# L2 norms of q and k: from the chunk loop of a gated DeltaNet block into its convolution stage

## The reference

```
proj = rms_norm(x) @ w_in
qkv  = silu(causal_depthwise_conv(concat(gq, gk, gv), conv_w))      # 4 taps
cq   = l2_normalize(q per head);  ck = l2_normalize(k per head)     # x * rsqrt(sum(x*x) + 1e-6)
g    = -exp(a_log) * softplus(ga + dt_bias);  beta = sigmoid(gb)
# in chunks, per head: decay = exp(differences of cumsum(g)), lower triangle
a_mat = I + strict_lower((k*beta) @ k.T * decay);  [u, w] = solve(a_mat, [v*beta, k*beta*exp(gc)])
v_new = u - w @ S;  o = (q*exp(gc)) @ S + lower(q @ k.T * decay) @ v_new
S     = S * exp(g_last) + (k * exp(g_last - gc)).T @ v_new
o_a   = o * rsqrt(mean(o*o) + 1e-6) * gdn_norm_w * silu(gz)
```

## Time and profile before

| | before |
|---|---|
| median of 3 runs | 1145.51 us |
| profiled execution, its own time | 1145.67 us |
| its span (first to last instruction) | 1143.9 us |
| PE busy | 1130.5 us (99%) |
| POOL / DVE / ACT busy | 540.0 / 526.8 / 454.2 us |
| mean granted TensorE clock | 0.998 of full |

### The profile page before, as it was taken

One profiled execution on the slowest core, in us unless ns is written; L12 is line 12 of the kernel. 1 busy time (PEld: TensorE's weight loads), 2 busy tenths in 40 slices (PEclk: granted clock), 3 DMA queues, 4 the chain that ended last, 5 costly groups with the idle time before them and its releaser, 6 DMA issues.

```text
span 1143.9 us, 16670 instructions
## 1 busy us (share of the span) xinstructions
PE 1130.5 (99%) x5955; PEld 948.3 (83%) x5955; DVE 526.8 (46%) x1136; ACT 454.2 (40%) x747; POOL 540.0 (47%) x326
## 2 busy tenths in 40 slices
PE   9999999999999999999999999999999999999997
PEld 8778888888888888888888888887888888888886
DVE  5344356464738257777777573413333333320001
ACT  6354453534444355555555432234332223221112
POOL 5344465362626165555555544434444444434443
PEclk9999999999999999999999999999999999999999
DMA  7233333131313254443444363532333333222231
GB/s 209 78 90 95 106 92 104 56 101 50 100 56 94 73 145 124 126 127 117 123 126 122 106 225 94 146 88 80 104 97 92 93 103 98 92 92 92 92 111 74
DMA packets 176177, 119.91 MB, mean 105 GB/s; under 512 B 6657, under 2 KB 164466, under 8 KB 176130
## 3 DMA queue, kind: packets, MB, share of 16 engines
q1 hardware_dynamic: 163088, 98.20, 29.5%
q10 hardware_dynamic: 13042, 21.07, 5.8%
HBM read 110.83 MB, written 8.42 MB: 104 GB/s over the span
## 4 chain that ended last, share of the span: by engine, by line
PE 87%; DVE 5%; issue 3%; POOL 2%; ACT 1%; DMA 1%; DVEq 0%; SPq 0%; POOLq 0%; ACTq 0%
PE ps L1542 62%; PE ps L1970 10%; PE ps L1650 6%; PE ps L1502 3%; PE ps L1862 2%; POOL w_lo L567 1%; PE ps L1833 1%; PE ps L1832 1%; DVE ps L1235 1%; DVE prod L1245 1%; PE ps L1906 1%; DVE Wb L1250 1%; DMA x_nat<-in_x 1%; PE ps L1592 0%; POOL rn L562 0%
## 5 line engine op out<-in xcount | busy, mean ns | idle before, releaser
L567 POOL TENSOR_TENSOR w_lo<-raw,w_hi 128x1024 fp32r<-128x1024 f32 x169 | 414.5, 2453 | 513.6 <-ACT w_hi L709 513.6
L1542 PE MATMUL ps<-h_hi,w_hi 128*128 128x512 f32 x976 | 384.1, 394 | 1.0 <-POOL w_lo L567 1.0
L1542 PE MATMUL ps<-h_lo,w_hi 128*128 128x512 f32 x976 | 383.0, 392 | 0.0
L1542 PE MATMUL ps<-h_hi,w_lo 128*128 128x512 f32 x976 | 382.7, 392 | 0.0
L709 ACT ACTIVATE w_hi<-raw 128x1024 fp32r<-128x1024 f32 x169 | 179.3, 1061 | 474.9 <-PE ps L1542 366.2
L1542 PEld LDWEIGHTS ps<-h_hi,w_hi 128*128 128x128 f32 x976 | 183.4, 188 | 38.8 <-issue 1.9
L1542 PEld LDWEIGHTS ps<-h_hi,w_lo 128*128 128x128 f32 x976 | 183.4, 188 | 37.7 <-issue 0.2
L1542 PEld LDWEIGHTS ps<-h_lo,w_hi 128*128 128x128 f32 x976 | 183.5, 188 | 36.1
L1111 DVE SCALAR_TENSOR_TENSOR tmp<-ps,prm,tmp 128x511 f32<-128x511 f32 (+2 forms) x72 | 53.9, 749 | 78.7 <-ACT tmp L745 73.4
L1065 DVE TENSOR_SCALAR ms<-ss 128x1 f32<-128x1 f32 x8 | 1.2, 153 | 123.5 <-ACT raw L1038 117.4
L1458 DVE TENSOR_TENSOR f_lo<-tmp,f_hi 128x512 f32 (+1 forms) x22 | 40.5, 1842 | 33.6 <-ACT f_hi L1011 33.6
(11 more groups left out here) (281 smaller groups left out, 1572.0 us busy)
## 6 DMA issues: line engine op xcount, KB each, us to landing
raw<-in_w_in SPq DMA_DIRECT2D x79, 512.0 KB, 3.8
raw<-in_w_gate SPq DMA_DIRECT2D x22, 512.0 KB, 3.7
raw<-in_w_up SPq DMA_DIRECT2D x22, 512.0 KB, 3.7
raw<-in_w_down SPq DMA_DIRECT2D x22, 512.0 KB, 3.4
gate_dram<-gate ACTq DMA_DIRECT2D x24, 256.0 KB, 2.0
cum<-cum_dram ACTq DMA_DIRECT2D x8, 512.0 KB, 7.4
raw<-in_w_branch_a SPq DMA_DIRECT2D x8, 512.0 KB, 4.4
raw<-in_w_branch_b SPq DMA_DIRECT2D x8, 512.0 KB, 4.0
```

Of the source, the lines that this page charges most:

```text
L567: pool.tensor_tensor(w_lo[:, r % 2, :], raw[:, r, :], w_hi[:, r % 2, :], ALU.subtract)\
L1542: return pe.matmul(ps[:, bank, :], wts[wl][k], acts[xl][:, k, :], start=(n == 0), stop=(n == len(PASSES) - 1))
```

## The change

Squares and sums of q and k are worked out while the convolution runs, for all 512 tokens, and without transposing q and k by PE:

- For units 0 to 15 (q and k), one unit late: behind the seed of unit u, ACT squares `qkv[:, u-1, :]` (128x512, into a buffer that alternates); behind the taps of unit u, DVE transposes it in blocks of 32x32 and sums each block row (128x512 to 128x16). Sixteen such results stand side by side in `sq_part`, 128x256.
- Before unit 18, PE multiplies `sq_part` once by four stacked 32x32 identities (`eye32`), which adds up the four block rows of each head: 32x256. After the taps of unit 19, DVE adds 1e-6 in four instructions, one for each 32 partitions, and puts them in place: `nsum`, 128 x 64 (4 chunks, 16 heads of q and k).
- POOL raises `nsum` to -1/2 in eight instructions of 128x8, all in the convolution stage. `decay_rows(0)` moves to behind the low part of unit 16.
- In the chunks, the transposes of q, the squares, the sums and the two powers are gone; bn, bn2 and c1 are made once for all chunks. k is transposed in chunks 0 to 2 only (for `Kd`).
- ACT's gate exponentials move from behind the SiLU of unit 5 to behind the seed of unit 6.
- The loops over the last units of the convolution on PE, ACT and DVE are written out.

```diff
# POOL
-            units(QKV0 + 1, NCONV // 4 - 1)
-            low_part(GATE0, 0)
-            low_part(GATE0, 1)
+            def row_powers(n):
+                pool.wait_ge(norm_ready, TT)
+                power(rn[:, n * H:(n + 1) * H], nsum[:, n * H:(n + 1) * H], H).then_inc(row_pow, 1)
+            units(QKV0 + 1, 3)
+            for r in range(4):
+                low_part(QKV0 + 4, r)
+                if r == 0:
+                    pool.wait_ge(g_split, 3)
+                    decay_rows(0)
+            for r in range(4):
+                low_part(QKV0 + 5, r)
+                row_powers(r)
+            low_part(GATE0, 0)
+            for n in range(4, 2 * TT):
+                row_powers(n)
+            low_part(GATE0, 1)
...
-            pool.wait_ge(g_split, 3)
-            decay_rows(0)
             ahead(0)
             decay_mask(0)
...
-                pool.wait_ge(k_sums, c + 1)
-                power(rn[:, H:2 * H], nsum[:, H:2 * H], H).then_inc(rk_ready, 1)
                 pool.wait_ge(masked, c + 1)
-                pool.wait_ge(row_step, c * 3 + 2)
-                pool.tensor_tensor(Eb[:, :, :], E[:, :, :], heads(bn2[:, :]), ALU.mult).then_inc(Eb_ready, 1)
+                pool.wait_ge(row_step, 2)
+                pool.tensor_tensor(Eb[:, :, :], E[:, :, :], heads(bn2[:, c * H:c * H + H]), ALU.mult)\
+                    .then_inc(Eb_ready, 1)
                 ahead(n - 1)
-                pool.wait_ge(q_sums, c + 1)
-                power(rn[:, 0:H], nsum[:, 0:H], H).then_inc(rq_ready, 1)
                 ahead(n)
# ACT, in conv(q, r), between the seed and the SiLU
+                if between:
+                    between()
+                u = 4 * q + r
+                if 0 < u <= 2 * H:
+                    act.wait_ge(conv_out, u)
+                    if u > 2:
+                        act.wait_ge(sq_turned, u - 2)
+                    act.activation(sq[(u - 1) % 2], qkv[:, u - 1, :], ACT.Square).then_inc(sq_made, 1)
...
-                if r == 1:
-                    act.wait_ge(small_taken, 3)
...
+                conv(1, r, False, gate_exps if r == 2 else None)
# DVE, in conv(q, r), behind the taps
+                u = 4 * q + r
+                if 0 < u <= 2 * H:
+                    dve.wait_ge(sq_made, u)
+                    if u > 1:
+                        dve.wait_ge(sq_summed_part, u - 1)
+                    dve.transpose(sq_blocks, sq[(u - 1) % 2]).then_inc(sq_turned, 1)
+                    dve.wait_ge(sq_turned, u)
+                    dve.tensor_reduce(sq_part[:, (u - 1) * 4 * TT:u * 4 * TT],
+                                      sq_blocks.rearrange("p (j d) -> p j d", d=LINE), AX.X, ALU.add)\
+                        .then_inc(sq_summed_part, 1)
...
+                    conv(q, r)
+                    if (q, r) == (4, 3):
+                        dve.wait_ge(norm_done, 1)
+                        sums_at = ps[0:LINE, 4, 0:2 * H * 4 * TT].rearrange("p (n c b) -> p b c n", c=TT, b=4)
+                        for b in range(4):
+                            dve.tensor_scalar(nsum[b * LINE:(b + 1) * LINE, :].rearrange("p (c n) -> p c n", c=TT),
+                                              sums_at[:, b], EPS, None, ALU.add).then_inc(norm_ready, 1)
# PE
-            with pe.Fori(3, NCONV // 4) as i:
+            for q in range(3, NCONV // 4):
                 for r in range(4):
-                    conv(i, r)
+                    if (q, r) == (4, 2):
+                        pe.wait_ge(eye_ready, 2)
+                        pe.wait_ge(sq_summed_part, 2 * H)
+                        pe.matmul(ps[0:LINE, 4, 0:2 * H * 4 * TT], eye32, sq_part, start=True, stop=True)\
+                            .then_inc(norm_done, 1)
+                    conv(q, r)
...
-                for a in range(2):
+                for a in range(2 if c < TT - 1 else 0):
                     per_head(a, lambda h, n: turn(bank4(a)[:, h, :], kT(n)), k_turned)
...
+                fill(FILLS[0])
                 pe.wait_ge(oT_ready, led(oT_ready, c * 2))
-                for a in range(2):
-                    per_head(a, lambda h, n: turn(bank4(2 + a)[:, h, :], qT(n)), q_turned)
-                fill(FILLS[0])
-                pe.wait_ge(q_squared, c * 2 + 2)
                 for a in range(2):
                     per_head(a, lambda h, n: mm(bank4(2 + a)[:, h, :], kT(n), kT(n)), G_done)
                 fill(FILLS[1])
-                pe.wait_ge(k_squared, c * 2 + 2)
```

More of the change, by code:

```diff
@@ L156, in hybrid_block @@
             cum = sb("cum", [FH, T])
[L157 to L162, removed]
+            nsum = sb("nsum", [P, TT * 2 * H])
+            rn = sb("rn", [P, TT * 2 * H])
+            bn = sb("bn", [P, TT * H])
+            bn2 = sb("bn2", [P, TT * H])
+            c1 = sb("c1", [P, TT * H])
             oss = sb("oss", [P, H])
@@ L169, in hybrid_block @@
             smT = Kd[0:64, 0:4, :].rearrange("p a n -> p (a n)")
+            sq = [o[:, 4 * a:4 * a + 4, :].rearrange("p h c -> p (h c)") for a in range(2)]
+            sq_blocks = Tm[:, 0:4, :].rearrange("p h c -> p (h c)")
+            sq_part = Tm[:, 4:6, :].rearrange("p h c -> p (h c)")
         with ExitStack() as part:
@@ L737, in _, with gate_exps, conv @@
             high_part(0, 1, True)
-            def conv(q, r, first=False):
+            def gate_exps():
+                act.wait_ge(small_taken, 3)
+                act.activation(gabs[:, :, :], gv[:, :, :], ACT.Abs).then_inc(gate_exp, 1)
+                act.wait_ge(gate_exp, 1)
+                act.activation(gabs[:, :, :], gabs[:, :, :], ACT.Exp, scale=-1.0).then_inc(gate_exp, 1)
+                act.activation(gb[:, :, :], gb[:, :, :], ACT.Exp, scale=-1.0).then_inc(gate_exp, 1)
+                act.activation(alog[:, :], alog[:, :], ACT.Exp).then_inc(gate_exp, 1)
+                act.wait_ge(gate_exp, 2)
+                act.activation(gabs[:, :, :], gabs[:, :, :], ACT.Ln, bias=1.0).then_inc(gate_exp, 1)
+            def conv(q, r, first=False, between=None):
                 high_ahead(q, r)
@@ L1155, in _ @@
                     copy(upto[:, :], step[:, 3 * P:4 * P]).then_inc(g_split, 1)
-            with dve.Fori(2, NCONV // 4) as i:
+                if r == 3:
+                    dve.tensor_reduce(eye32, ident[:, :].rearrange("p (q j) -> p j q", q=4), AX.X, ALU.add)\
+                        .then_inc(eye_ready, 1)
+            for q in range(2, NCONV // 4):
                 for r in range(4):
-                    conv(i, r)
+                    conv(q, r)
[5 more added lines that the diff above has]
+                                              sums_at[:, b], EPS, None, ALU.add).then_inc(norm_ready, 1)
             dve.wait_ge(consts_ready, 16)
```

90 lines of the change are left out of this document (35 added, 55 removed).

## The result

The changed kernel takes 1154.78 us, the median of 6 runs (1153.02 to 1157.78), against 1145.49 us for the kernel before, measured beside it (6 runs, 1145.25 to 1146.05). The ratio is 1.0085, with a 95% interval of 1.0075 to 1.0095: it is 9.3 us slower. The forecast was 1144.3 us and its range ended at 1147.2. It was wrong.

What follows compares the result with a forecast made beforehand. PE, busy 99% of the span, was taken as the bound. Savings of 8.1 us against 6.85 us of new work and waits gave -1.25 us: 1144.3 us, range 1142.0 to 1147.2.

Steps and rivals of the forecast that it cites:

- Step 1: Chunks, on PE: 40 transposes gone, 32 for q and 8 for k in chunk 3, saving 4.2 us.
- Step 2: Convolution, unit 8: moving ACT's gate exponentials removes PE's wait for its low part, saving 1.0 us.
- Step 3: Chunk 0: PE's wait for the decay rows goes, since POOL makes them behind unit 16's low part; saves 0.7 us.
- Steps 5 and 6: Before unit 18: the identity product adds 0.45 us on PE, and PE's wait for DVE's sum before it 0.5 us.
- Step 7: Unit 21: its low part stands behind POOL's first power, which waits for nsum; a new PE wait of 3.9 us.
- Step 8: Unit 25: four POOL powers in a row delay its low part; a second PE wait of 2.0 us.
- Step 4: Chunks 0 to 2: DVE gains about 2.4 us, so all PE waits for Zm go, saving 2.2 us.
- Rival A: Unit 21's new wait: the clock falls, costing 1.7 to 3.4 us more, 1146.0 to 1147.7 us; chance 0.22.
- Rival B: Units 21 and 25: POOL's waits far smaller than forecast; 1138.4 us if powers don't delay unit 21; chance 0.14.
- chunks that don't shorten: Stated sign of error; chunks should shorten by 0.84 us plus their former Zm wait, chunk 3 by 1.7 us.

Runs made afterwards that it cites:

- turns_back: Changed kernel with POOL's powers later, DVE's bn, Lq, Wb earlier, identity product before unit 19, and the 40 removed transposes issued again, unused: 1142.42 us, ratio 0.9974.
- bn_early: Changed kernel with each POOL power behind the next unit's low part and DVE's bn, bn2, c ahead of chunk 0's decay cut: 1138.71 us, ratio 0.9943.
- pool_waits: Changed kernel with three POOL waits in chunk 0: mask behind bn rows, Eb behind Lq, low part of unit 28 behind Lc: 1146.60 us, ratio 1.0011.
- both_warm: Changed kernel with unread identity transposes on PE, 34 ahead of chunk 0's Zm wait and 30 ahead of unit 21's wait: 1149.11 us, ratio 1.0033.

## Why the prediction was wrong, step by step

- **Step 1** (-4.2): right. Chunk 0 has 16 transposes in 1.91 us where the earlier trace rows has 24, and turns_back gives 4.3.
- **Step 2** (-1.0): right, -1.2 alone.
- **Step 3** (-0.7): right, the wait is gone.
- **Steps 5 and 6** (+0.45, +0.5): right. The block transpose took 0.71 us and the sum 0.69 (DVE's timeline), near the 0.65 and 0.67 taken; the wait was 0.5.

```profile
29.62 0.71 DVE L1138 STREAM_TRANSPOSE Tm<-o 128x512 f32<-128x512 f32 x1 [0.15 <-DVE tmp L1127]
30.36 0.69 DVE L1140 TENSOR_REDUCE Tm<-Tm 128x16 f32<-128x512 f32 x1
```

- **Step 7** (+3.9): right as a wait; its clock was not in the sum. POOL's timeline shows the chain as worked out:

```profile
135.95 1.65 POOL L564 TENSOR_TENSOR rn<-nsum,half_neg 128x8 f32<-128x8 f32 x1 [7.06 <-DVE nsum L1192]
137.56 2.35 POOL L569 TENSOR_TENSOR w_lo<-raw,w_hi 128x1024 fp32r<-128x1024 f32 x1
```

- **Step 8** (+2.0): 1.6.
- **Step 4** (-2.2): this is the step that failed; it put POOL's hold on DVE at nothing. It says that "DVE gains about 2.4 us". By the timelines of PE and DVE, the stretch from PE's decay product to DVE's first shuffle was 177.64 - 160.07 = 17.6 us before and 187.92 - 166.70 = 21.2 after: it *lost* 3.6. I took every remaining DVE instruction at its old duration. But those durations held only for the old places: by luck of the releases they began ahead of POOL's long instructions, between them, or beside a power. Without the reductions and the power between them, `bn`, `Wb`, `Lq` and `Lc` came up behind the start of POOL's instructions of 1.9 to 2.4 us and stood still for 6.8 us. Without those 6.8 us the stretch would be 3.2 us shorter than before, by these numbers, so the 2.4 was not too much for what step 4 did count. The wait in chunk 0 became 4.8 us and in chunk 1 1.1: +5.9 - 2.2 = +3.7 instead of -2.2. One of the stated signs of being wrong, chunks that don't shorten, came with it in chunk 0.
- **Rival A** (0.22) held the second failure. It named the right place and mechanism, and its cost for one gap (1.7 to 3.4) contains the 1.7 of the rows. I gave it too little: the one fall in the rows came 3.4 us behind PE's last work, the new wait was 3.7 by my own working, and I took "hardly longer" as a reason against. And step 4 made a second such gap, which no rival had. "TensorE: Matmul & The Clock Gate", section "HAM oscillation", of the Trainium skill, which the prediction cited and set against its sum, has a long enough idle gap of PE put it back to the slow level. Both gaps, of 3.9 and 4.8 us, agree.

The profiled sum, by the steps: -4.2 - 1.0 - 0.7 - 2.2 + 0.45 + 0.5 + 5.5 + 5.9 = +4.25, and 1.7 + 6.7 for the clock: +12.6 against 12.1 by the table of stretches. In the median the clock's part is smaller, 4 to 5 us.

**Rival B** was right about what the change is worth without its side effects. It gave 1138.4 with no waits on low parts, by the same sum in which all of the `Zm` wait goes; bn_early, with no wait on a low part and 0.6 us of `Zm` wait left, has 1138.7. The reason it gave, that the powers might not hold back unit 21, was not so: they did, by 3.9 us.

What stays open: why the clock stays low for longer behind the second gap than behind the first, and for a different time from run to run; and why POOL's powers do not hold DVE up.

## What to carry to other kernels

When a change takes instructions out of one engine's queue, don't only subtract them: the ones behind them get new neighbours on the engine that shares SBUF with theirs. Look for two-operand DVE rows whose duration is near a POOL row's, and give one side a wait, or start the DVE side first. And price any new PE wait of about 4 us twice, once as the wait and once as the clock's fall behind it; if it can't be removed, let PE turn something in it.

## What was not expected of the hardware

- A DVE product over 128x32 elements took 0.19 us or 2.26, one over 128x256 0.41 or 2.6. In chunk 0 of the changed kernel each long one had begun 0.05 to 0.3 us behind the start of a POOL instruction over 128x1024, and with POOL held back in pool_waits they were short again.
- POOL's powers over 128x8 (1.65 us) did not hold up DVE's `Lc`, a product of two operands in SBUF: in the four chunks of the kernel before it took 0.29 to 0.32 us, begun 0.03 to 0.06 us behind a power. In chunk 0 it took 0.31 us from 175.88, while this power ran:

```profile
175.84 1.65 POOL L562 TENSOR_TENSOR rn<-nsum,half_neg 128x8 f32<-128x8 f32 x1
```

- PE's identity transposes kept the clock at 1.00 through both gaps (both_warm).
- The fall does not need PE to be still idle when it comes. In the changed kernel the window in which PE was idle from 138 to 140 had 1.00, and the fall came with PE back at work. At the second gap it came while PE was idle.
